# Layer 1 of block 1 projects in three rounded passes, with the weights' high and low parts made on GpSimd and ScalarE

## The reference

```python
xn = _rms_norm(x, g_norm) * (1 + sc[:, None]) + sh[:, None]
cn = _rms_norm(ctx, g_norm) * (1 + sc_c) + sh_c
(au, av, az, bq, bk, bv, bz, cq, ck, cv, co, cz, cg) = _split_proj(xn @ w_in)
(au_c, av_c, az_c, bq_c, bk_c, bv_c, bz_c, cq_c, ck_c, cv_c, co_c, cz_c, cg_c) = _split_proj(cn @ w_in)
```

## Time and profile before

| | us |
|---|---|
| runs, median | 1822.85 |
| runs, lowest and highest | 1815.21, 1823.6 |
| the profiled execution | 1806.77 |
| its span, first to last instruction | 1805.0 |
| TensorE busy | 1574.0 (87%) |
| VectorE busy | 1007.2 (56%) |
| ScalarE busy | 680.9 (38%) |
| GpSimd busy | 296.2 (16%) |

### The profile page before, as it was taken

One profiled execution on the slowest core, in us unless ns is written; L12 is line 12 of the kernel. 1 busy time (PEld: TensorE's weight loads), 2 busy tenths in 40 slices (PEclk: granted clock), 3 DMA queues, 4 the chain that ended last, 5 costly groups with the idle time before them and its releaser, 6 DMA issues.

```text
span 1805.0 us, 19092 instructions
## 1 busy us (share of the span) xinstructions
PE 1574.0 (87%) x7341; PEld 1154.8 (64%) x7341; DVE 1007.2 (56%) x1527; ACT 680.9 (38%) x1081; POOL 296.2 (16%) x278
## 2 busy tenths in 40 slices
PE   5988986779899677799888999888999898989998
PEld 2767762454655434477677777647888676657886
DVE  1318446651457554466465674627777454247776
ACT  2311127211211331456114551124666466335664
POOL 1546620000000000444113441000000042000000
PEclk8899998869899877899688998898999799889999
DMA  8655411200565320666364665307988341039983
GB/s 309 238 160 180 172 47 51 68 1 0 176 238 195 137 94 12 198 211 211 117 168 153 214 215 147 94 0 257 309 297 277 133 157 64 1 118 323 303 289 110
DMA packets 186470, 290.69 MB, mean 161 GB/s; under 512 B 13739, under 2 KB 95115, under 8 KB 186380
## 3 DMA queue, kind: packets, MB, share of 16 engines
q1 hardware_dynamic: 171936, 272.93, 44.7%
q0 software_dynamic: 13200, 13.03, 3.2%
q10 hardware_dynamic: 1244, 3.52, 0.5%
HBM read 287.96 MB, written 1.49 MB: 160 GB/s over the span
## 4 chain that ended last, share of the span: by engine, by line
PE 65%; DVE 21%; ACT 8%; issue 2%; DMA 2%; SPq 1%; POOL 0%; ACTq 0%; DVEq 0%
PE ps L1110 27%; PE ps L2419 13%; DVE P L1791 3%; DVE acc L1833 3%; PE ps L2329 3%; PE ps L1291 2%; ACT ps L1680 2%; DVE PT L1791 2%; PE ps L1272 2%; PE ps L2437 2%; PE ps L2438 1%; PE ps L2439 1%; DVE E L1791 1%; PE ps L1280 1%; DVE small L2025 1%
## 5 line engine op out<-in xcount | busy, mean ns | idle before, releaser
L1110 PE MATMUL ps<-WB,YP 128*128 128x512 f32 x1152 | 279.7, 401 | 19.8 <-DVE WB L1791 19.8
L1110 PEld LDWEIGHTS ps<-WB,YP 128*128 128x128 f32 x1152 | 218.2, 192 | 72.5 <-issue 15.6
L1791 DVE TENSOR_TENSOR WP<-ring,WP 128x2048 fp32r<-128x2048 f32 x96 | 218.8, 2290 | 50.1 <-ACT WP L691 50.0
L1110 PE MATMUL ps<-WP,XP 128*128 128x512 f32 x960 | 233.2, 396 | 8.2 <-DVE WP L1791 8.2
L1110 PEld LDWEIGHTS ps<-WP,XP 128*128 128x128 f32 x960 | 178.8, 189 | 46.0 <-DVE WP L1791 9.3
L691 ACT ACTIVATE WP<-ring 128x2048 fp32r<-128x2048 f32 x96 | 183.3, 1914 | 38.2 <-PE ps L1110 38.2
L2419 PE MATMUL ps<-ring,XT 128*128 128x512 f32 (+3 forms) x448 | 167.3, 530 | 5.5 <-ACT XT L1616 3.3
L562 POOL TENSOR_TENSOR WB<-ring,WB 128x512 fp32r<-128x512 f32 x96 | 133.8, 1396 | 188.9 <-ACT WB L621 188.9
L621 ACT ACTIVATE WB<-ring 128x512 fp32r<-128x512 f32 x192 | 113.9, 628 | 74.9 <-PE ps L1110 72.4
L1833 DVE SCALAR_TENSOR_TENSOR acc<-ring,silu_c,acc 128x512 f32<-128x512 f32 x168 | 138.1, 822 | 5.4
L1791 DVE TENSOR_TENSOR WB<-ring,WB 128x512 fp32r<-128x512 f32 x96 | 85.6, 896 | 97.9 <-ACT WB L621 97.1
(11 more groups left out here) (337 smaller groups left out, 2309.0 us busy)
## 6 DMA issues: line engine op xcount, KB each, us to landing
ring<-in_w_ada SPq DMA_DIRECT2D x72, 1024.0 KB, 7.4
ring<-in_a_w_in SPq DMA_DIRECT2D x36, 1024.0 KB, 5.2
ring<-in_w_gate SPq DMA_DIRECT2D x64, 512.0 KB, 4.5
ring<-in_w_up SPq DMA_DIRECT2D x64, 512.0 KB, 5.6
ring<-in_w_down SPq DMA_DIRECT2D x32, 1024.0 KB, 6.7
ring<-in_w_in SPq DMA_DIRECT2D x24, 1024.0 KB, 7.1
ring<-in_b_w_in SPq DMA_DIRECT2D x12, 1024.0 KB, 5.4
ring<-in_w_out SPq DMA_DIRECT2D x8, 1024.0 KB, 5.1
```

Of the source, the lines that this page charges most:

```text
L1110: ins = mm(dst, x(a), w(b), start=(start and n == 0), stop=(stop_ and n == 2))
L1791: return v.tensor_tensor(out_, a, b, op)
```

## The change

Layer 1 now projects with `project_split` as well. ScalarE and VectorE make `XH` and `XL` again for layer 1. GpSimd's loop over the 56 blocks becomes `weight_parts(l)` and runs a second time, after `x_tile` has reached 4. The high parts of chunks 2, 3 and 6 of layer 1 (24 of 56) are made by ScalarE, in `highs`, which stands ahead of the evictions of the same chunk; the low parts all stay with GpSimd. On ScalarE the tanh of silu(AZ) moves from behind the evictions of chunk 2 to behind those of chunk 3, and that of CO from behind the evictions of chunk 5 to behind the high parts of chunk 6; VectorE's order is unchanged. A pair of ring slots of layer 1 is no longer released as a whole when its chunk is complete, but the first half after block 3. The one line left out of the diff declares the semaphore `win_hi`.

```diff
@@ -308,7 +308,7 @@
 
 
         released, units, outs, dve_items, ada_items, mixed = [], 0, 0, 0, 0, 0
-        units_at = {}
+        units_at, chunk_units = {}, {}
         for n, it in enumerate(flat):
             kind = it[0]
             if kind == "ada":
@@ -322,10 +322,11 @@
             first = len(it) < 5 or it[4] == 0
             if kind == "win":
                 if first:
-                    units += T if it[1] == 0 or CTX_LAST[CHUNKS.index(it[2:4])] else 2
-                    if it[1] == 0:
-                        released.append(("win_used", 7 * CHUNKS.index(it[2:4]) + 4))
-                        continue
+                    ch = CHUNKS.index(it[2:4])
+                    units += T if it[1] == 0 or CTX_LAST[ch] else 2
+                    chunk_units[it[1], ch] = units
+                    released.append(("win_used", 49 * it[1] + 7 * ch + 4))
+                    continue
             elif kind in ("awin", "bwin"):
                 if first:
                     units += 2
@@ -502,17 +503,28 @@
             return slot(it)[:, 512 * (k % 4):512 * (k % 4) + 512], it
 
         rounded = split("rounded", 400, p_at + 4 * 12672)
-        def win_block(q):
+
+        HI_BY_ACT = (2, 3, 6)
+
+        def win_block(l, q):
 
             lo, hi = CHUNKS[q // 8]
             w, k = hi - lo, q % 8
-            it = index[("win", 0, lo, hi, k // 4)]
+            it = index[("win", l, lo, hi, k // 4)]
             cols = slice((k % 4) * w, (k % 4) * w + w)
             return it, slot(it)[:, cols], WH[:, q % 4, 0:w], WL[:, it % RING, cols]
 
-        def win_block_used(q):
-
-            return ("win_used", 7 * (q // 8) + q % 8 + 1) if q % 8 < 7 else ("proj", T * (q // 8 + 1))
+        def win_block_used(l, q):
+
+            return ("win_used", 49 * l + 7 * (q // 8) + q % 8 + 1) if q % 8 < 7 else ("proj", chunk_units[l, q // 8])
+
+        def hi_by_act(l, q):
+
+            return l == 1 and q // 8 in HI_BY_ACT
+
+        def hi_count(q):
+
+            return sum(hi_by_act(1, n) for n in range(q + 1))
 
         jrev = rounded[:, 0:128]
         ident_r, causal, both = rounded[:, 0:128], [rounded[:, 128:256], rounded[:, 256:384]], rounded[:, 384:400]
@@ -1480,28 +1492,39 @@
 
             chained = 1
 
-            def high(q):
+            def high(l, q):
 
                 nonlocal chained
-                it, w, hi, _ = win_block(q)
+                it, w, hi, _ = win_block(l, q)
+                if hi_by_act(l, q):
+                    return
                 if q % 4 == 0:
                     item_ready(pool, it)
                 if q >= 4:
-                    name, value = win_block_used(q - 4)
+                    name, value = win_block_used(l, q - 4)
                     pool.wait_ge(S(name), value)
                 nc.gpsimd.tensor_copy(hi, w).then_inc(S("chain_pool"), 1)
                 chained += 1
 
-            high(0)
-            for q in range(56):
-                if q < 55:
-                    high(q + 1)
-                pool.wait_ge(S("chain_pool"), chained - (q < 55))
-                _, w, hi, lo = win_block(q)
-                nc.gpsimd.tensor_tensor(lo, w, hi.bitcast(F32), ALU.subtract).then_inc(S("win_lo"), 1)
+            def weight_parts(l):
+
+                high(l, 0)
+                for q in range(56):
+                    before = chained
+                    if q < 55:
+                        high(l, q + 1)
+                    if hi_by_act(l, q):
+                        pool.wait_ge(S("win_hi"), hi_count(q))
+                    else:
+                        pool.wait_ge(S("chain_pool"), before)
+                    _, w, hi, lo = win_block(l, q)
+                    nc.gpsimd.tensor_tensor(lo, w, hi.bitcast(F32), ALU.subtract).then_inc(S("win_lo"), 1)
 
             for l in range(2):
                 tiles = slice(0, T) if l == 0 else slice(2, T)
+                if l == 1:
+                    pool.wait_ge(S("x_tile"), T)
+                weight_parts(l)
                 for half, w in enumerate((CQ, CV)):
                     pool.wait_ge(S("bz_tanh"), 2 * l + half + 1)
                     e, x = P[:, tiles, w:w + 256], P[:, tiles, BZ + 256 * half:BZ + 256 * half + 256]
@@ -1655,12 +1678,15 @@
                     silu_part(CZ, CZ + 256, L, Ef)
                 elif ci == 2:
                     rstd_small(hr, hs, HD)
-                    silu_part(AZ, AZ + 256, L, Ef)
+                    if l == 0:
+                        silu_part(AZ, AZ + 256, L, Ef)
                 elif ci == 3:
+                    if l == 1:
+                        silu_part(AZ, AZ + 256, L, Ef)
                     for t in range(0, len(L), 2):
                         gelu_part(L[t:t + 2])
                     rstd_small(lnv, lnv, HD)
-                elif ci == 5:
+                elif ci == 5 and l == 0:
                     silu_part(CO, CO + 256, L, Ef)
 
             def exponentials(u, cols):
@@ -1720,10 +1746,23 @@
                 norm(range(T), lambda s: A1[:, l, s, :], lambda s: M1[:, l, s, 0:8], mods=l + 1)
                 if l == 0:
                     act.wait_ge(S("hk_out"), 16)
-                    for k in range(KB):
-                        act.wait_ge(S("xt_act" if k % 2 == 0 else "xt_dve"), k // 2 + 1)
-                        s_.activation(XH[:, k], XT[:, k], ACT.Copy).then_inc(S("xt_hi"), 1)
+                for k in range(KB):
+                    act.wait_ge(S("xt_act" if k % 2 == 0 else "xt_dve"), 4 * l + k // 2 + 1)
+                    s_.activation(XH[:, k], XT[:, k], ACT.Copy).then_inc(S("xt_hi"), 1)
+
+                def highs(ch):
+                    for q in range(8 * ch, 8 * ch + 8) if l == 1 and ch in HI_BY_ACT else ():
+                        it, w, hi_, _ = win_block(l, q)
+                        if q % 4 == 0:
+                            item_ready(act, it)
+                        name, value = win_block_used(l, q - 4)
+                        act.wait_ge(S(name), value)
+                        s_.activation(hi_, w, ACT.Copy).then_inc(S("win_hi"), 1)
+
                 for k, (lo, hi) in enumerate(CHUNKS):
+                    highs(k)
+                    if l == 1 and k == 6:
+                        silu_part(CO, CO + 256, L, Ef)
                     for t in range(T):
                         rng = (lo, hi) if (t >= 2 or l == 0) else CTX_LAST[k]
                         if rng:
@@ -2135,10 +2174,9 @@
             def block1(l):
                 L = list(range(T)) if l == 0 else list(LAT)
                 norm(range(T), lambda s: A1[:, l, s, :], lambda s: M1[:, l, s, 0:8])
-                if l == 0:
-                    for k in range(KB):
-                        dve.wait_ge(S("xt_hi"), k + 1)
-                        tt(XL[:, k], XT[:, k], XH[:, k].bitcast(F32), ALU.subtract).then_inc(S("xt_lo"), 1)
+                for k in range(KB):
+                    dve.wait_ge(S("xt_hi"), 8 * l + k + 1)
+                    tt(XL[:, k], XT[:, k], XH[:, k].bitcast(F32), ALU.subtract).then_inc(S("xt_lo"), 1)
                 for k, (lo, hi) in enumerate(CHUNKS):
                     for kind, layer, ch in MODS_BEHIND[l].get(k, ()) if l == 1 else ():
                         ada(kind, layer, ch)
@@ -2420,23 +2458,24 @@
                                  start=(half == 0 and k == 0), stop=(half == len(its) - 1 and k == kk - 1))
                 return ins
 
-            def project_split(n):
-
-                w = CHUNKS[n][1] - CHUNKS[n][0]
-                us = [c.up("proj") - 1 for _ in range(T)]
+            def project_split(l, n):
+
+                lo, hi = CHUNKS[n]
+                parts = [(t, (lo, hi) if l == 0 or t >= 2 else CTX_LAST[n]) for t in range(T)]
+                parts = [(t, slice(r[0] - lo, r[1] - lo), c.up("proj") - 1) for t, r in parts if r]
                 for k in range(KB):
                     q = 8 * n + k
-                    _, _, hi, lo = win_block(q)
+                    _, _, high, low = win_block(l, q)
                     if n == 0:
-                        pe.wait_ge(S("xt_lo"), k + 1)
-                    pe.wait_ge(S("win_lo"), q + 1)
-                    for t in range(T):
-                        if k == 0 and us[t] >= 4:
-                            pe.wait_ge(S("evict"), us[t] - 3)
-                        b, cols = bank(us[t] % 4, 0, w), slice(128 * t, 128 * t + 128)
-                        mm(b, XH[:, k, cols], hi, start=(k == 0), stop=False)
-                        mm(b, XH[:, k, cols], lo, start=False, stop=False)
-                        ins = mm(b, XL[:, k, cols], hi, start=False, stop=(k == KB - 1))
+                        pe.wait_ge(S("xt_lo"), 8 * l + k + 1)
+                    pe.wait_ge(S("win_lo"), 56 * l + q + 1)
+                    for t, r, u in parts:
+                        if k == 0 and u >= 4:
+                            pe.wait_ge(S("evict"), u - 3)
+                        b, cols = bank(u % 4, 0, r.stop - r.start), slice(128 * t, 128 * t + 128)
```

(11 more changed lines are left out.)

2 lines of the change are left out of this document (1 added, 1 removed).

## The result

| us | before | after |
|---|---|---|
| runs, median | 1819.03 | 1843.65 |
| runs, lowest and highest | 1810.45, 1823.6 | 1837.81, 1854.86 |
| the profiled execution, its span | 1806.77, 1805.0 | 1843.57, 1841.7 |

The change makes the kernel slower: the ratio is 1.0138, its 95% interval 1.0108 to 1.0169, four runs of each. Between the medians lie 24.6 us.

The account below looks back on a forecast made before the run. It took TensorE to bound layer 1's projection stage (126.8 us) and expected hand-overs and GpSimd-VectorE collisions to lengthen it by 21 us; from the median 1822.85 it forecast 1843, range 1826 to 1860.

Parts of the forecast that it names:

- the sum of +21: Layer 1's projections: chunk 0 +1, chunks 1 and 2 -2, chunk 3 +9, 4 +1, 5 +9, 6 and end +3 us.
- The gain on TensorE: Layer 1's projections: three passes cost 0.68 us against 0.86 for the fp32 matmul; possible gain some 20 us of 126.8.
- if the blocks are always there in time: Condition on the possible gain of some 20 us: weight parts always ready for TensorE in layer 1's projections.
- The bound "no collision": If GpSimd and VectorE did not collide at all, the stage ends near 591.5: -4.5 us, 1818 in all.
- Chunk 0: First chunk of layer 1's projections: starts 470.4, 9.8 us at the low clock, ends 486.4 against 485.5; +1 us.
- Chunks 2 and 3: Late starts behind ScalarE's queue, low parts in turns with VectorE: 14.4 and 15.1 us; some 7 us idle before chunk 3.
- Chunks 4 and 5: Tanh of AZ at 547.3, chunk 4's evictions at 578; TensorE starts chunk 5 at 578.3, not 558.30; +1 and +9 us.
- some 11 us of idling: TensorE's wait before chunk 5 for ScalarE's evictions of chunk 4; the low clock after it costs 2 us more.
- The signs named ahead: Profile after: GpSimd some 80 us busier, low parts near 1.5 us, modulation steps near 1.3, idling before chunks 3 and 5.
- The turns are not hidden: Judges the rival that turns are mostly hidden in TensorE's slower chunks: 0 to +8 us, near 1826; chance 0.17.
- The faster case: Rival: no chunk starts late, chunk 4's evictions within 1 us of its last matmul; -15 us, 1808; chance 0.07.
- Whole operations waiting for each other: Rival: GpSimd and VectorE each wait for the other's whole operation, low parts 2 us apart; +32 us, 1855; chance 0.13.

Follow-up runs that it names:

- the bare load: Kernel before plus GpSimd copies and subtractions of the same shapes on constants that nobody waits for; ratio 1.0085, stage 151.6 us.
- The kernel with fewer sums: Changed kernel without six of the eight modulation steps in each of the stage's seven items; ratio 1.0089, stage 146.5 us.
- The passes alone: Changed kernel making no weight parts in layer 1, four filled buffers reused: ratio 0.9962, stage 122.9 us; with chunk 0 wide too, 0.9899, 114.9 us.
- The kernel with wide passes: Changed kernel with chunk 0 of layer 1 at 272 columns instead of 16 for the two context tiles; ratio 1.0094, stage 147.0 us.
- The kernel with all edits: Changed kernel with wide chunk 0, early chunk 4 evictions, three early high parts, low part ahead of next chunk's high part; ratio 1.0067, stage 142.9 us.

## Why the prediction was right, and where its steps missed

**The mechanism held; that the number hit is in part luck.** The forecast was a slower kernel with a median of 1843, in a range of 1826 to 1860; 1843.65 was measured. The 1843 were made of 1822.85, the median of three runs before, and the sum of +21. With a fourth run the median of the kernel before is 1819.03, 3.8 lower, and the medians lie 24.6 apart, 3.6 more than forecast: the two errors cancel. The profiled execution was forecast at 1828 and took 1843.57; the 16 us that I added from there to the median were 12.3 in the kernel before and 0.1 in this one. The chunks' own times give -1.1 for chunks 1 and 2 and +8.3 for chunk 5 where the sum has -2 and +9, with the same total. That GpSimd and VectorE block each other is shown from both sides: take the parts away and the multiply-adds have their 752 ns again and the stage takes 122.9; add the bare load to the kernel before and they have 1084, and its stage grows by 24.8. The kernel with fewer sums agrees with this less well: it gave up 7 us where collisions were to give up 13 to 18.

**The gain on TensorE** was there, but smaller. The forecast priced TensorE alone at 93.7 us, plus seven sums of 0.8 and the clock's share, a possible gain of some 20. The passes alone gave 114.9 with the early clock, of which 7.7 are the wait for the layer norm, so 107.2 and a gain of 19.6; with the clock as it came in the changed kernel they gave 122.9, without that wait 115.2 and a gain of 11.6. The step "if the blocks are always there in time" left that chain out; without the parts TensorE still waits for it. The bound "no collision" in the prediction (-4.5 us) has this chain and comes close to the measured -3.9 (122.9 against 126.8), but partly by chance: it counts hand-overs that the kernel without parts does not have, and not the long low clock.

**Chunk 0, the mis-sized term.** I took the low clock's 9.8 us from the kernel before. It was low for some 25 us, so chunk 1 ended at 40.05 us behind the first matmul instead of 32.6 (503.0 - 470.4): 7.5 us later, and nearly all the later forecasts are too early by about this amount. In the profiled stage the sum should be +21 and was +27.9 (26.6, and 1.3 for the later first matmul). So this is the term of the sum that was mis-sized: 9.8 us of low clock forecast, 25.6 measured. The whole stage came out 6.9 us longer than forecast, counted from its first matmul (153.4 instead of 616.9 - 470.4 = 146.5). The kernel with wide passes names the cause: they give 8.1 us back there and 6.4 at the end.

**Chunks 2 and 3.** The idle time before chunk 3 was forecast as about 7 us, released by GpSimd's low part; it was 7.49 <-POOL, for the reason given: ScalarE's square root at 539.00 waits for VectorE's sums of squares, and the roundings stand behind it. Eight low parts of chunk 2 in 14.4 us were forecast, 13.35 measured (518.02 to 531.37).

**Chunks 4 and 5: two misses that cancel.** The tanh of AZ was forecast 76.9 us behind the first matmul and came at 90.2 (566.79 - 476.58). 7.5 of the 13.3 are the clock's; the rest is q and k, which suffered more than I gave them, because copies collide too (below). But from the tanh to the evictions of chunk 4 it took 590.21 - 566.79 = 23.4 us, not 30.7. The reason is in GpSimd's and VectorE's timelines:

First GpSimd's:

```profile
568.50 1.73 POOL L1521 TENSOR_TENSOR WL<-ring,WH 128x512 fp32r<-128x512 f32 x1
578.01 0.67 POOL L1506 CAST WH<-ring 128x512 fp32r<-128x512 f32 x1 [7.77 <-DMA ring<-in_w_in]
578.65 2.24 POOL L1521 TENSOR_TENSOR WL<-ring,WH 128x512 fp32r<-128x512 f32 x1
```

And VectorE's:

```profile
570.55 5.47 DVE L1872 SCALAR_TENSOR_TENSOR acc<-ring,silu_c,acc 128x512 f32<-128x512 f32 x7
```

GpSimd waits 7.77 us for the weights of chunk 5, whose load came late because its slot in the ring was held by a modulation item (chunk 3's) that VectorE began only at 569.12, behind q and k. Meanwhile seven multiply-adds run at 0.78 each. And the last low part of chunk 4 is queued behind this waiting high part, so TensorE's last block of chunk 4 is late by 8.29 us. I had not seen that step, although the rows of the queue show it (a `CAST` with `slot_full_4` ahead of a `TENSOR_TENSOR`). It took over 8.29 of the "some 11 us of idling" before chunk 5; ScalarE's eviction accounts for 5.18 only. It did not decide, since the root came later still, at 590.00 against 584.59 for the end of chunk 4. The kernel with all edits takes this order away, and the wait inside chunk 4 with it; what the order costs alone was not run.

**The signs named ahead.** GpSimd was to be busy for some 80 us more: 100.5. Low parts near 1.5 us: 1482 ns. Modulation steps near 1.3 us: 1043 ns, less than said: for GpSimd waits in places for the hand-over and for loads (18.4 and 7.8 us in its groups above), and fourteen of the 49 ran at 0.78, seven in such a gap and seven behind its last low part. TensorE's idling before chunk 5 was to be some 10 us, released by the eviction: it is 5.18, with 8.29 more for the low part inside chunk 4. Chunk 5 was forecast 107.9 us behind the first matmul (578.3 - 470.4), and a start before 94.6 (565 - 470.4) would have refuted it: 114.1. Before the last sums TensorE waited 3.28 us for VectorE's last multiply-add, behind the silu of CO, as forecast.

**The rivals.** The turns are not hidden: the waits stand in the timeline. The faster case needed the evictions of chunk 4 within 1 us of its last matmul; they came 5.6 us after its sums began (590.21 - 584.59). Whole operations waiting for each other would have put the low parts of chunks 2 and 3 some 2 us apart, 2.02 for a low part and a multiply-add; they were 13.35 / 8 = 1.67 us apart in chunk 2, the multiply-adds 11.81 / 7 = 1.69, less even than the 1.80 that I took from two pairs, and in chunk 3 the first five low parts 7.03 / 5 = 1.41. The Trainium skill ("SBUF — State Buffer", Who interferes with whom) says that whoever comes first has the shared ports for the whole instruction. It names the right engines; the estimate of 2.02 us for a pair that follows from it with the durations of the rows (1.27 + 0.75) is above what they show.

**What is open.** The price of 30.5 us for the parts is not split exactly: the experiments share it between the hand-over of ScalarE (6), the modulation (7) and the rest of VectorE's work with the chain behind it, and such shares need not add up. The ratio of the load alone makes 15 us where its profiled stage grows by 24.8; behind the stage, where the edit changes nothing, the profiled executions take from 1201.0 us (this one) over 1209.0 (the kernel before) to 1220.4 (fewer sums in the kernel before), so one execution's total does not settle it, and it stays open. That the ring slot was held by VectorE's item is read from one trace, not shown by a kernel of its own.
